# A decoder step on one core: x loaded once and later, its squares summed by GpSimd, gate rows in four column groups, memory keys 512 columns at a time

## The reference

```python
def rms_norm(x, g):
    y = xf * lax.rsqrt(jnp.mean(xf * xf, axis=-1, keepdims=True) + EPS)
    return y * g
# memory_kv
mn = rms_norm(mem, norm_mem)
k = rms_norm((mn @ wk).reshape(B, N_MEM, X_HEADS, X_HD), k_norm)
# trunk_layer
proj = rms_norm(x, p['norm_mix']) @ p['w_in']
qk_m, v_m, o_m, ig, fg, q_a, k_a, v_a = jnp.split(proj, idx, axis=-1)
```

## Time and profile before

| what | value |
|---|---|
| median of 3 runs | 1361.61 us (1361.06 to 1362.67) |
| profiled execution | 1361.21 us, span 1359.4 us |
| PE busy | 1330.2 us, 98% |
| weight loads of PE | 1300.6 us, 96% |
| DVE busy | 819.1 us, 60% |
| ACT busy | 621.7 us, 46% |
| POOL busy | 97.4 us, 7% |
| DMA | 251.87 MB, mean 185 GB/s |

### The profile page before, as it was taken

One profiled execution on the slowest core, in us unless ns is written; L12 is line 12 of the kernel. 1 busy time (PEld: TensorE's weight loads), 2 busy tenths in 40 slices (PEclk: granted clock), 3 DMA queues, 4 the chain that ended last, 5 costly groups with the idle time before them and its releaser, 6 DMA issues.

```text
span 1359.4 us, 27260 instructions
## 1 busy us (share of the span) xinstructions
PE 1330.2 (98%) x10213; PEld 1300.6 (96%) x10213; DVE 819.1 (60%) x1240; ACT 621.7 (46%) x889; POOL 97.4 (7%) x139
## 2 busy tenths in 40 slices
PE   7999999999999998999999999999999999999999
PEld 7998989878999987999999999999999999999999
DVE  7767888787666466665444565444565444565443
ACT  7674666667444455543333343333343333343331
POOL 0032000121422202000000000000000000000000
PEclk9999999999999999999999999999999999999999
DMA  9677444765944963645544545544545544545543
GB/s 381 248 227 254 135 138 137 237 208 173 374 157 160 283 229 109 213 158 170 170 159 165 163 160 171 170 160 164 164 161 169 169 160 165 167 159 169 170 158 128
DMA packets 75276, 251.87 MB, mean 185 GB/s; under 512 B 8332, under 2 KB 17376, under 8 KB 74560
## 3 DMA queue, kind: packets, MB, share of 16 engines
q1 hardware_dynamic: 59184, 215.49, 46.0%
q0 software_dynamic: 15744, 35.07, 8.2%
q10 hardware_dynamic: 288, 0.48, 0.1%
HBM read 238.00 MB, written 13.63 MB: 185 GB/s over the span
## 4 chain that ended last, share of the span: by engine, by line
PE 83%; DVE 8%; ACT 3%; DMA 3%; issue 2%; ACTq 0%; SPq 0%; DVEq 0%
PE g L520 79%; PE m L520 3%; DVE arena L1453 3%; DMA raw<-in_stream 2%; ACT arena L992 2%; DVE wlo L1467 2%; DVE arena L1450 1%; ACT whi L1010 1%; DMA arena<-arena 1%; DVE b_lo L1453 0%; ACT a_hi L992 0%; DMA arena<-in_memT 0%; DVE arena L1442 0%; DVE arena L1446 0%; DVE small L1733 0%
## 5 line engine op out<-in xcount | busy, mean ns | idle before, releaser
L1467 DVE TENSOR_TENSOR wlo<-raw,whi 128x1024 fp32r<-128x1024 f32 x388 | 476.0, 1237 | 375.8 <-ACT whi L1010 363.9
L1010 ACT ACTIVATE whi<-raw 128x1024 fp32r<-128x1024 f32 x388 | 408.0, 1059 | 477.2 <-PE g L520 440.7
L520 PE MATMUL g<-a_hi,whi 128*128 128x288 f32 x1632 | 355.3, 299 | 1.5 <-ACT a_hi L992 1.5
L520 PE MATMUL g<-a_lo,whi 128*128 128x288 f32 x1632 | 349.5, 295 | 0.0
L520 PE MATMUL g<-a_hi,wlo 128*128 128x288 f32 x1632 | 348.2, 295 | 0.0
L520 PE MATMUL g<-b_hi,whi 128*128 128x288 f32 x1344 | 288.9, 296 | 5.6 <-DVE arena L1450 5.3
L520 PE MATMUL g<-b_lo,whi 128*128 128x288 f32 x1344 | 287.8, 295 | 0.0
L520 PE MATMUL g<-b_hi,wlo 128*128 128x288 f32 x1344 | 287.0, 295 | 0.0
L520 PEld LDWEIGHTS g<-a_hi,whi 128*128 128x128 f32 x1632 | 260.6, 188 | 8.3 <-issue 5.2
L520 PEld LDWEIGHTS g<-a_hi,wlo 128*128 128x128 f32 x1632 | 261.6, 187 | 0.0
L520 PEld LDWEIGHTS g<-a_lo,whi 128*128 128x128 f32 x1632 | 261.5, 188 | 0.0
(11 more groups left out here) (181 smaller groups left out, 693.9 us busy)
## 6 DMA issues: line engine op xcount, KB each, us to landing
raw<-in_stream SPq DMA_DIRECT2D x388, 512.0 KB, 3.5
arena<-in_state_C POOLq DMA_DIRECT2D x8, 512.0 KB, 5.8
out_s_C<-arena POOLq DMA_DIRECT2D x8, 512.0 KB, 3.8
arena<-in_kdT POOLq DMA_DIRECT2D x8, 512.0 KB, 17.2
arena<-in_cache_mem_v POOLq DMA_DIRECT2D x8, 512.0 KB, 8.7
arena<-in_xT SPq DMA_DIRECT2D x4, 576.0 KB, 8.5
arena<-in_xT POOLq DMA_DIRECT2D x1, 2304.0 KB, 10.5
arena<-in_memT SPq DMA_DIRECT2D x4, 512.0 KB, 7.0
```

The costliest lines, as they stand in the source:

```text
L520: return pe.matmul(out, lhsT, rhs, start=start, stop=stop, skip_group_check=True)
L1010: act.activation(whi[:, s], raw[:, s], ACT.Copy).then_inc(sem["hi_done"], 1)
L1467: dve.tensor_tensor(wlo[:, s], raw[:, s], f32(whi[:, s]), SUB).then_inc(sem["chunk_split"], 1)
```

## The change

The memory keys' chunks are laid anew: two rows of features by 512 columns, so that `mem_chunk` runs 12 matmuls of 512 columns per chunk into G[2] and G[3], and each row is final only with chunk 7. DVE evicts them then, in four copies. Chunk 0 and the memory come in smaller pieces; four matmuls of zeros stand ahead (`warm`). x is loaded behind chunks 6 to 9, `x_prep` moves with it, and the second load is gone. POOL squares the first half of x and ACT the second half, POOL adds all (`xacc`), and two matmuls of ones sum over features. The gate rows are sixteen fp32 matmuls of 32 output rows from raw x, four sums abreast in PE's column groups, with the gain folded into `wgs`; two matmuls then add the four (`gates_sum`). `gates_a` has four instructions fewer, which is not shown.

```diff
+    out = [w["wk_x"][0][r:r + 2 * P].reshape(2, P, 2, CW).transpose(0, 2, 1, 3).reshape(CK * P, CW)
+           for r in range(0, D, 2 * P)]
...
-            for b in range(4):
+            def mem(b):
+                load(memT[:, 2 * b:2 * b + 2, :], ins["memT"][:, 2 * b:2 * b + 2, :], sem["mem_in"][b])
+
+            half = 2 * CW
+            load(raw[:, 0, 0:2].rearrange("p a b -> p (a b)"), ins["stream"][0][:, 0:half], sem["raw_ready"][0])
+            mem(0)
+            load(raw[:, 0, 2:4].rearrange("p a b -> p (a b)"), ins["stream"][0][:, half:2 * half], sem["first_raw"])
+            for b in range(1, 4):
                 chunk(b, ins["stream"][b], None)
-                load(memT[:, CK * b:CK * b + CK, :], ins["memT"][:, CK * b:CK * b + CK, :], sem["mem_in"][b])
-            for b in range(4):
-                chunk(b, ins["stream"][RING + b], b + 1)
+                mem(b)
+            mem(4)
+            def x_load(b):
                 load(xT[:, CK * b:CK * b + CK, :], ins["xT"][:, CK * b:CK * b + CK, :], sem["x_in"][b])
-                if b == 1:
+
+            for c in range(RING, 4 * RING):
+                chunk(c % RING, ins["stream"][c], c - RING + 1)
+                if c < 7:
+                    mem(c + 1)
+                if c == 6:
+                    x_load(0)
+                if c == 7:
                     load(wg_raw[:, :, :], ins["gates"], sem["wg_in"])
-            for c in range(2 * RING, 4 * RING):
-                chunk(c % RING, ins["stream"][c], c - RING + 1)
-                j = c - 2 * RING
-                if j == 0:
-                    sp.wait_ge(sem["mem_hi"], 16)
-                    sp.wait_ge(sem["mem_lo"], 16)
-                if 2 <= j < 4:
-                    load(xtok[:, j - 2, :], ins["x_prompt"][0, (j - 2) * P:(j - 1) * P, :], sem["xtok_in"][j - 2])
-                if j == 3:
-                    load(xdec, ins["x_quarters"], sem["xtok_in"][2])
-                if j == 0:
+                if 7 <= c < 10:
+                    x_load(c - 6)
+                if c == 9:
                     load(cst[:, :], consts, sem["cst_in"])
...
-        for kt in range(12, KT):
-            beside[0].append(("mem_prep", kt))
+        for kt in range(6, KT):
+            beside[kt // 2 - 3].append(("mem_prep", kt))
         for kt in range(KT):
-            beside[2 + kt // 2].append(("x_prep", kt))
+            beside[(5, 5, 6, 6, 7, 7, 8, 8, 8, 9, 9, 9, 10, 10, 10, 11)[kt]].append(("x_prep", kt))
         beside[7].append(("gate_weights",))
-        for j in range(3):
-            beside[10 + j].append(("x_squares", j))
-        for c, what in ((12, "norm_x"), (12, "gates_mm"), (13, "gates_a"), (14, "gates_ln"), (15, "gates_b"),
+        for j in range(8):
+            beside[(7, 7, 8, 8, 9, 10, 11, 11)[j]].append(("x_squares", j))
+        for c, what in ((11, "gates_mm"), (12, "norm_x"), (12, "gates_sum"), (13, "gates_a"), (14, "gates_ln"), (15, "gates_b"),
...
+            def warm():
+                pe.wait_ge(sem["dve_once"], before["warm_ready"] + 1)
+                for _ in range(4):
+                    mm(M[3][:, 0:256], rstd[:, 0:P], rstd[:, 0:256])
+            def mem_chunk(c):
+                if c:
+                    pe.wait_ge(sem["chunk_split"], c + 1)
+                s = c % RING
+                for k in range(2):
+                    kt = 2 * c + k
+                    if c == 0:
+                        pe.wait_ge(sem["first_hi"] if k == 0 else sem["hi_done"], 1)
+                    pe.wait_ge(sem["mem_hi"], kt + 1)
+                    for i, (w, a) in enumerate(((whi, act_hi[1]), (whi, act_lo[1]), (wlo, act_hi[1]))):
+                        if i == 1:
+                            pe.wait_ge(sem["mem_lo"], kt + 1)
+                        if i == 2 and c == 0:
+                            pe.wait_ge(sem["first_lo"] if k == 0 else sem["chunk_split"], 1)
+                        for j in range(2):
+                            m = mm(G[2 + j][:, :], a[:, kt, j * P:(j + 1) * P],
+                                   w[:, s, 2 * k:2 * k + 2, :].rearrange("p a b -> p (a b)"), kt == 0 and i == 0,
+                                   kt == KT - 1 and i == 2)
+                            if kt == KT - 1 and i == 2 and j == 0:
+                                m.then_inc(sem["tile0_done"], 2)
+                m.then_inc(sem["chunk_used"], 1)
...
             def norm_x():
                 pe.wait_ge(sem["cst_in"], 16)
-                pe.wait_ge(sem["dve_once"], before["diag_ready"] + 3)
-                mm(M[0][:, 0:NT], ones, diag).then_inc(sem["pe_once"], 1)
+                pe.wait_ge(sem["x_add"], 8)
+                mm(M[0][:, 0:NT], ones, xacc[:, 0, :], True, False)
+                mm(M[0][:, 0:NT], ones, xacc[:, 1, :], False, True).then_inc(sem["pe_once"], 1)
             def gates_mm():
-                pe.wait_ge(sem["dve_once"], before["wg_split"] + 3)
-                for kt in range(KT):
-                    half, k = divmod(kt, 8)
-                    w = wgx[:, half, MH * k:MH * k + P]
-                    for i, a in enumerate((act_hi, act_lo)):
-                        m = mm(M[1][:, 0:NT], w, a[0][:, kt, :], kt == 0 and i == 0, kt == KT - 1 and i == 1)
+                pe.wait_ge(sem["dve_once"], before["wg_split"] + 2)
+                for k in range(4):
+                    for i in range(4):
+                        m = mm(M[1][32 * i:32 * i + 32, 0:NT], wgs[:, 4 * k + i, :], xT[:, 4 * k + i, :], k == 0, k == 3)
                 m.then_inc(sem["pe_once"], 1)
+
+            def gates_sum():
+                pe.wait_ge(sem["act_once"], before["gsum_out"] + 1)
+                mm(M[2][0:32, 0:NT], cst[:, C_SEL:C_SEL + 32], gsum)
+                mm(M[2][32:64, 0:NT], cst[:, C_SEL + MH:C_SEL + MH + 32], gsum).then_inc(sem["pe_once"], 1)
...
             def x_squares(j):
-                act.wait_ge(sem["xtok_in"][j], 16)
-                x = xtok[:, j, :] if j < 2 else xdec
-                A(x, x, ACT.Square, accum_out=sm_(SSX + j)).then_inc(sem["act_once"], 1)
-                act.wait_ge(sem["act_once"], now("x_ssq"))
+                if j < 4:
+                    return
+                act.wait_ge(sem["x_in"][j // 2], 16)
+                act.wait_ge(sem["mem_lo"], 5)
+                act.wait_ge(sem["x_add"], j - 1)
+                A(xq2[j % 2], xT[:, 2 * j:2 * j + 2, :], ACT.Square).then_inc(sem["act_once"], 1)
+                act.wait_ge(sem["act_once"], now("x_sqr"))
+            def gates_mm():
+                act.wait_ge(sem["pe_once"], before["gates_part"] + 1)
+                A(gsum, M[1][:, 0:NT]).then_inc(sem["act_once"], 1)
+                act.wait_ge(sem["act_once"], now("gsum_out"))
...
             def gate_weights():
                 dve.wait_ge(sem["wg_in"], 16)
-                copy(wgx[:, :, 0:64], wg_raw[:, :, 0:64]).then_inc(sem["dve_once"], 1)
+                dve.memset(wgs, 0.0).then_inc(sem["dve_once"], 1)
                 dve.wait_ge(sem["dve_once"], now("wg_split"))
-                copy(wgx[:, :, 128:160], wg_raw[:, :, 64:96]).then_inc(sem["dve_once"], 1)
+                tt(wgs[:, :, 0:2 * MH], wg_raw[:, :, :], gcol[:, 0:KT].unsqueeze(2).to_broadcast([P, KT, 2 * MH]),
+                   MUL).then_inc(sem["dve_once"], 1)
                 dve.wait_ge(sem["dve_once"], now("wg_split"))
-                tt(wgx[:, :, 64:128], wg_raw[:, :, 0:64], f32(wgx[:, :, 0:64]), SUB).then_inc(sem["dve_once"], 1)
...
-                if c % 4 == 3 and c // 4 != KVA or c == 4 * KVA + 4:
+                if c == 4 * KVA - 1:
+                    for j in range(2):
+                        if j == 0:
+                            dve.wait_ge(sem["tile0_done"], 2)
+                        else:
+                            dve.wait_ge(sem["chunk_used"], 8)
+                        for half in range(2):
+                            copy(kvm[:, j, half * CW:(half + 1) * CW],
+                                 G[2 + j][:, half * CW:(half + 1) * CW]).then_inc(sem["tile_out"], 1)
+                            dve.wait_ge(sem["tile_out"], now("tile_out"))
+                elif c > 4 * KVA and c % 4 == 3 and c // 4 != KVA or c == 4 * KVA + 4:
...
-                        if q < KVA:
-                            copy(kvm[:, j, q * CW:(q + 1) * CW], g[:, 0:CW]).then_inc(sem["tile_out"], 1)
-                            dve.wait_ge(sem["tile_out"], now("tile_out"))
-                        elif QKM <= q < OM and (q - QKM) % 2 == 0:
+                        if QKM <= q < OM and (q - QKM) % 2 == 0:
...
+            for j in range(8):
+                if j == 0:
+                    pool.wait_ge(sem["mem_hi"], 5)
+                    pool.wait_ge(sem["mem_lo"], 5)
+                if j < 4:
+                    pool.wait_ge(sem["x_in"][j // 2], 16)
+                    x = xT[:, 2 * j:2 * j + 2, :]
+                    if j == 0:
+                        pool.tensor_tensor(xacc, x, x, ALU.mult).then_inc(sem["x_add"], 1)
+                    else:
```

(37 more changed lines are left out.)

63 lines of the change are left out of this document (25 added, 38 removed).

## The result

The changed kernel takes 1374.5 us (median of 4 runs, 1373.48 to 1375.73) against 1361.73 for the kernel before: 1.0098 of its time, 95% interval 1.0086 to 1.0109, or 12.8 us more by the medians. 1366.0 was forecast, with 1361.0 to 1369.2 as the range. The direction was right, the size was not: a rise of 4.75 was forecast.

The account below looks back on a forecast made before the run. The prediction took TensorE (PE) as the full engine, so only its start, waits and time between count. 1361.21 + 6.05 - 4.8 + 1.5 + 1.2 + 0.8 = 1366.0 us, range 1361.0 to 1369.2.

Parts of the forecast that it names:

- start of chunk 8: PE's first matmul of x waits for DVE's copies of the memory keys: 38.2 instead of 32.15 us, +6.05.
- chunks 8 to 11: half clock and late rows: Behind PE's wait: matmuls at half clock, +1.5, and the last row of x prepared late, +1.2.
- norm and gates: Between chunks 12 and 13: 8.52 us of wait, norm and gate matmuls become 3.74, -4.8.
- k_norm: Behind chunk 15: PE waits because DVE's gate rows come later than ACT is ready, +0.8, between 0 and 1.5.
- Every sign that the prediction named: Short first wait, 8 to 10 us at chunk 8 (37 to 40), longer DVE rows, lower clock, chunk 12 to 13 under 2.
- from 19.3 to 31.4: Ahead of chunk 8: seven GpSimd and seven DVE instructions take turns at the ports, 12.0 us in all.
- The data bound: Chunk 10's landing plus 5.1 us of ACT and DVE work would let chunk 8 start at 35.1 to 36.5.
- Step (b): In chunk 11, the last row of x is late behind split 14, with one or two GpSimd adds against it: +1.2.
- rival C: Squares at the add's price, GpSimd first, chunk 8 at 39.7, clock toll also behind later stalls: 1369.2, chance 0.10.
- Rival D: At chunk 12 PE waits for GpSimd's last add: +1 to +2 on the forecast, chance counted within its 0.56.
- Rival A: No port contest: GpSimd's squares run beside DVE, chunk 8 starts when data allows, 35.1 to 36.5; 1363, chance 0.20.
- Rival B: Faster: chunk 10 lands by 27 to 28, DVE copies nearly in time, chunk 8 at 32 to 33; 1357.5, chance 0.14.

## Why the prediction was wrong, step by step

| step | forecast | measured |
|---|---|---|
| start of chunk 8 | +6.05 | +8.05 |
| chunks 8 to 11: half clock and late rows | +2.7 | +5.7 (18.57 us instead of 4 x 3.22) |
| norm and gates | -4.8 | -3.5 |
| k_norm | +0.8 | +0.5 |
| behind k_norm | 0 | +1.6 |
| sum | +4.75 | +12.3 |

The mechanism of the large term was right: PE waits at chunk 8 for the copies, DVE is behind, and GpSimd holds it by turns. Every sign that the prediction named came, with chunk 8 0.2 past its 37 to 40. Three terms were too favourable: the start of chunk 8 by 2.0, chunks 8 to 11 by 3.0, norm and gates by 1.3.

**Chunk 8, 2.0 short.** The step that failed is "from 19.3 to 31.4". I let DVE stand at the low parts of row 12 when x landed, without adding up its own list. It came there at 21.60, and the seven rows ended at 33.18 (the first a_lo) instead of 31.4. x landed later than forecast too (GpSimd begins at 21.00), but the experiment with whole pieces shows that a landing 1.4 earlier doesn't help. The length of the contest, 12.0 forecast and 12.2 measured, from 21.00 to 33.18, is partly luck: GpSimd's seven instructions cost 9.34 where 8.5 stood (a square 1.21, 1.05 taken), DVE's seven rows 4.97 (written as 4.9), and 2.1 us of both lie side by side instead of 1.4. The data bound was rightly seen as the lesser one: with the squares cut, chunk 8 is at 37.4, where I had 35.1 to 36.5; ACT takes chunk 10 there at 32.03, not at 31.4.

**Chunks 8 to 11, 3.0 short: late rows, and the clock a second time.** This is the largest miss. Step (b) took only the last row of x and "one or two" adds: 1.2. Three rows were late, 2.78 in all, of which the last four adds make 2.0 and the order 0.76 (0.6 without adds was forecast); some 0.6 more are lost around these three waits. Behind the wait of 9.4 sixteen matmuls, from 40.20 to 44.1, took 0.24 instead of 0.13, half of full speed again: 1.8 (1.5 forecast). Behind the wait of 1.80 ahead of row 15 PE ran at half clock once more: 0.6 in the last six matmuls of chunk 11, and then in the gate matmuls. A second stretch at half clock I had given to rival C alone. The granted clock of the changed kernel from 57.3 to 62 us is 0.64, and 1.00 at the same work with the squares cut (columns as in the earlier trace rows):

```profile
57.30:62.00 4.70, 4.63 (x38) 2.38 (x38) 0.00 (x0) 0.00 (x0) 1.20 (x1) 0.64 0.26 100
```

```profile
52.40:57.00 4.60, 4.59 (x49) 3.29 (x50) 0.00 (x0) 1.31 (x2) 0.22 (x1) 1.00 0.41 118
```

That the wait of 1.80 brings it is likely, not shown. The two other kernels with this wait have the same fall (0.69 with the copies moved, 0.68 with whole pieces), but without the wait at chunk 8 the clock stays at 1.00 behind a wait of 2.38 at this place.

**Norm and gates, 1.3 short.** The price of 2.1 for the gate matmuls was right at full clock: 2.15 in seven of the experiments, 2.16 in an eighth. In the changed kernel they ran at half clock, 3.24, and that is 1.1 of the 1.3.

**k_norm** cost 0.5, of which 0.21 is a wait; 0.8 was a little much (8.1 - 7.2, from which it came, is 0.9). Rival D did not occur: the norm didn't wait for GpSimd's last add.

**Behind k_norm** I had 0 and the profiled execution shows 1.6. It can be placed: 1.0 by 132 us, where PE waits 1.19 for a copy of DVE instead of 0.26, and 1.5 from 276 to 280 us, where PE runs at half clock behind a wait of 1.77 (granted clock 0.66 from 275 to 280 us) and before ran at full clock behind one of 2.12; some 0.9 comes back in shorter waits. The windows around it, of the changed kernel and of before:

```profile
250.00:300.00 50.00, 47.64 (x365) 41.75 (x364) 37.87 (x84) 30.62 (x61) 9.86 (x16) 0.97 0.74 228
```

```profile
238.00:288.00 50.00, 46.94 (x370) 40.81 (x368) 38.64 (x85) 31.13 (x61) 9.81 (x16) 1.00 0.71 230
```

The other profiled executions show between -0.4 and +3.7 there, without an order that follows the edits, and that of gates_a ahead of the evictions has a fall of the clock at the same place. So this term is at least in part chance of the execution; why the wait at 132 us is longer stays open.

Rival A, no contest, is refuted: with the contest gone DVE's rows shrink from 2.66 to 1.00. Rival B needed chunk 10 before 28 us; DVE itself was at 36. Rival C came nearest, with the second stretch at half clock, but is 5 us short as well. The Trainium skill, "SBUF — State Buffer", section "SBUF: two separate sides", would have both engines take turns for whole instructions. Here seven rows of DVE (4.97 alone) and seven of GpSimd (4 x 1.21 + 3 x 1.50 = 9.34) would then need 14.3; they took 12.2, from 21.00 to the end of the first a_lo at 33.18. By this measurement the exclusion holds in kind, but on average 0.3 us of each GpSimd row lies beside the next one of DVE (the profile's spans of GpSimd are rough).

## What to carry to other kernels

When a wait is moved, add up the whole list of the engine that it waits for, from its first idle row on; the landing of the data alone gives a time that is too early. Work handed to an idle GpSimd wasn't free here, where the busy DVE reads two SBUF inputs: price it as DVE time. Of a bundle of edits one may well gain: run the parts singly (here the gate groups, 2.5 us by the medians).

## What the runs showed of the hardware

PE's first matmuls run at half speed, and for how long differs between executions of nearly the same program. Their pairs of 256 columns follow each other by 0.43 us, and by 0.24 later. The change comes at 10.5 us in the profiled execution of before, but at 13.0 in that of gates_a ahead of the evictions and at 13.1 with GpSimd's instructions on the kernel before. The first of these two views is of before:

```profile
10.49 0.57 PE L520 MATMUL g<-whi,b_hi 128*128 128x256 f32 x2
10.89 0.40 PE L520 MATMUL g<-whi,b_lo 128*128 128x256 f32 x2
```

```profile
12.56 0.63 PE L517 MATMUL g<-whi,b_lo 128*128 128x256 f32 x2
12.99 0.52 PE L517 MATMUL g<-wlo,b_hi 128*128 128x256 f32 x2
13.35 0.40 PE L517 MATMUL g<-whi,b_hi 128*128 128x256 f32 x2
```

The granted clock of the profile doesn't show this stretch: it is 1.00 from 8 to 13 us in all three, unlike behind the later waits. Why stays open.

The time of an execution goes with its mean granted clock. Runs of the kernel before lay between 1359.3 and 1364.5: in the largest set, of 29, fourteen at 1.000 have a median of 1359.95 and six at 0.997 one of 1362.52. So a gain of 1.6 can be lost in a median. Among executions at 1.000 alone, gates_a ahead of the evictions (1357.46, three) is 1.4 ahead of the gate groups alone (1358.87, six), just what its account expected, and those are 1.3 ahead of the kernel before (1360.12, five). These are few executions, sorted afterwards: a sign, nothing shown. A kernel that waits less may also lose less clock, and such a gain is left out of this comparison.

The changed kernel's pairs of 512 columns follow each other by 0.46 us from 6.95 on, full speed, behind zeros that run from 1.36 us; no run leaves the zeros out. The earlier start brings nothing here, since DVE needs until 40 us all the same.
